# Two pieces of TensorE work taken across stage ends: half of an output product, and a first forward transform

## What is computed

```python
for l in range(DEPTH):                               # DEPTH = 2
    ux = modulate(hx, norm1_g[l], sh1x, sc1x)
    px = ux @ w_in[l]
    ...
    att_x = latent_attention(...)
    hy_x = hyena_branch(px[..., :HY_COLS], sc_w[l], sc_b[l], flt, flt_bias[l])
    hx = hx + g1x * merge_branches(px[..., MLA_END:], hy_x, att_x, w_hy_o[l], w_mla_o[l], w_out[l])
    ...
    hx = hx + g2x * hier_moe(modulate(hx, norm2_g[l], sh2x, sc2x), *moe_w)

def hyena_branch(p_hy, sc_w, sc_b, flt, flt_bias):
    u = short_conv(p_hy, sc_w, sc_b)
    v, x1, x2 = jnp.split(u, 3, axis=-1)
    z = v
    for o, gate in enumerate((x1, x2)):
        z = gate * (long_conv(z, h_freq[:, o]) + flt_bias[o] * z)
    return z

def merge_branches(p_gate, y_hy, y_att, w_hy_o, w_mla_o, w_out):
    g = jax.nn.sigmoid(p_gate)
    return (g[..., :D_MODEL] * (y_hy @ w_hy_o) + g[..., D_MODEL:] * (y_att @ w_mla_o)) @ w_out
```

## Time and profile before

| | us |
|---|---|
| median of three runs | 2640.35 |
| the three runs | 2635.67, 2640.35, 2643.16 |
| the profiled execution | 2635.22 |
| its span | 2633.4 |
| TensorE busy in it | 2422.3 (92%) |
| VectorE busy | 1073.3 (41%) |
| GpSimd busy | 691.3 (26%) |
| ScalarE busy | 621.5 (24%) |
| main transfer queue, share of 16 engines | 55.5% |
| granted TensorE clock, mean | 0.981 of full speed |

### The profile page before, as it was taken

How to read it: one execution, slowest core, us unless ns; L and a number is a source line. 1 busy time by engine, 2 the same in 40 slices (tenths; PEclk the granted TensorE clock), 3 DMA queues, 4 the chain that set the end, 5 groups by cost and what they waited for, 6 DMA issues and landing times. The chain is left out here.

```text
span 2633.4 us, 35470 instructions
## 1 busy us (share of the span) xinstructions
PE 2422.3 (92%) x13020; PEld 1519.3 (58%) x13020; DVE 1073.3 (41%) x2144; ACT 621.5 (24%) x1374; POOL 691.3 (26%) x644
## 2 busy tenths in 40 slices
PE   7999988999999999998888899999999999988887
PEld 3455675555555565555554468645787665555553
DVE  5764487444212663111111175944422732222222
ACT  4441122442110232221111142234211311111111
POOL 0003132565221012222221222246431022222221
PEclk9999999999999999999999999999999999999999
DMA  9982020021113539999999913012226599999996
GB/s 365 372 343 92 28 95 19 14 55 25 48 48 94 233 137 391 395 398 400 402 392 385 360 41 116 33 32 55 49 73 208 233 361 395 392 408 404 403 402 242
DMA packets 192142, 588.40 MB, mean 223 GB/s; under 512 B 48464, under 2 KB 110203, under 8 KB 135708
## 3 DMA queue, kind: packets, MB, share of 16 engines
q1 hardware_dynamic: 167525, 551.99, 55.5%
q0 software_dynamic: 22400, 29.42, 3.4%
q10 hardware_dynamic: 2103, 5.51, 0.5%
HBM read 581.44 MB, written 51.51 MB: 240 GB/s over the span
## 5 line engine op out<-in xcount | busy, mean ns | idle before, releaser
L2661 PE MATMUL ps<-w,moe_xt 128*64 128x256 f32 x2816 | 341.2, 397 | 61.3 <-DMA w<-in_w_up_e 59.0
L2801 POOL DMA_INDIRECT rows_out<-moe_rows_out,table x128 | 117.9, 921 | 738.5 <-DVE moe_rows_out L2866 375.1
L2661 PEld LDWEIGHTS ps<-w,moe_xt 128*64 128x64 f32 x2816 | 221.3, 142 | 150.8 <-issue 67.6
L2916 DVE TENSOR_TENSOR moe_gated<-ps,moe_gated 64x256 f32<-64x256 f32 x128 | 54.5, 426 | 501.0 <-ACT moe_gated L2885 500.9
L2885 ACT ACTIVATE moe_gated<-ps 64x256 f32<-64x256 f32 x128 | 48.2, 376 | 666.9 <-PE ps L2661 666.9
L2661 PE MATMUL ps<-early_w,moe_xt 128*64 128x256 f32 x1280 | 153.4, 394 | 28.3 <-DMA early_w<-in_w_up_e 28.3
L1706 POOL TENSOR_SCALAR attn_p<-attn_p,attn_rs 128x768 f32<-128x768 f32 (+1 forms) x80 | 155.4, 1951 | 81.2 <-DVE attn_rs L1880 80.7
L2669 PE MATMUL ps<-w,moe_ht 128*64 128x512 f32 x704 | 170.4, 604 | 2.3 <-issue 2.3
L2178 PE MATMUL ps<-w_out,mix 128*128 128x512 f32 x320 | 144.6, 602 | 7.0 <-PEq L150 7.0
L2902 DVE TENSOR_TENSOR moe_rows_out<-ps,moe_row_gate 64x512 f32<-64x512 f32 x128 | 88.1, 688 | 138.3 <-PE ps L2669 136.2
L2661 PEld LDWEIGHTS ps<-early_w,moe_xt 128*64 128x64 f32 x1280 | 101.8, 141 | 65.9 <-issue 31.7
(11 more groups left out here) (435 smaller groups left out, 4271.8 us busy)
## 6 DMA issues: line engine op xcount, KB each, us to landing
w<-in_w_gate_e SPq DMA_DIRECT2D x88, 1024.0 KB, 25.9
w<-in_w_up_e SPq DMA_DIRECT2D x88, 1024.0 KB, 29.5
w<-in_w_down_e SPq DMA_DIRECT2D x88, 1024.0 KB, 29.3
prep_w<-in_w_ada SPq DMA_DIRECT2D x24, 2048.0 KB, 16.0
early_w<-in_w_gate_e SPq DMA_DIRECT2D x40, 1024.0 KB, 25.7
early_w<-in_w_up_e SPq DMA_DIRECT2D x40, 1024.0 KB, 29.5
early_w<-in_w_down_e SPq DMA_DIRECT2D x40, 1024.0 KB, 29.7
w_merge<-in_w_in SPq DMA_DIRECT2D x32, 512.0 KB, 5.4
```

The source lines that it names most:

```text
L2661: last = nc.tensor.matmul(ps[k * SLOTS:(k + 1) * SLOTS, 0:DE], xt[:, c], wgu[:, k, c], start=c == 0, stop=c == KC - 1)
L2801: nc.gpsimd.indirect_dma_start(out=dram["y"], out_offset=bass.IndirectOffsetOnAxis(ap=m.table[0:SLOTS, j:j + 1], axis=0), in_=y[:, j % 2], ...
L2916: nc.vector.tensor_tensor(h[:, b % 2], m.ps[SLOTS:2 * SLOTS, b % 2, 0:DE], sg[SLOTS:2 * SLOTS, b % 2], ALU.mult).then_inc(s["h_done"], 1)
```

## The change

Two pieces of TensorE's work are issued in the stage ahead of the one that uses them.

First, the forward transform of job 0 becomes a function `long_forward` and is issued at the end of `hyena_in_stage`, in place of the 16 small matmuls. Before it, TensorE waits for the matrix `dft0`, for the last copies into `m.v`, and for VectorE's last additions out of banks 0 to 3. `forward(0)` in `conv_stage` is left with counting `fwd_done`.

Second, the first half (chunks 0 to 3 of 8) of the first half-product of `out_stage` is issued at the end of `merge_stage`, by a function `out_product` that both stages use. Before it, TensorE waits for the first half of `w_out`, for seven of the eight sums into `m.mix`, and for the last addition out of bank 0. In `out_stage`, tile 0 begins with chunk 4.

```diff
-def hyena_in_stage(nc, m, l, w_in, streams, early, latent, then):
+def hyena_in_stage(nc, m, l, w_in, streams, early, latent, dft0, then):
...
-            keep_warm(nc, m, 4, 16)
+            dft, dft_in = dft0
+            pe.wait_ge(dft_in, 16)
+            pe.wait_ge(s["tr_evac"], 2 * HC)
+            pe.wait_ge(s["u3_done"], NP)
+            pe.wait_ge(s["u2_done"], NP)
+            pe.wait_ge(s["c22_done"], NP)
+            pe.wait_ge(s["c21_done"], NP)
+            long_forward(nc, m, dft, m.v, 0, 0)
...
+def long_forward(nc, m, dft, src, tok0, half):
+
+    cols = slice(half * (HW // 2), (half + 1) * (HW // 2))
+    for e, residue in enumerate(FORWARD):
+        last = nc.tensor.matmul(m.ps[:, e // 2, (e % 2) * (HW // 2):(e % 2 + 1) * (HW // 2)], dft[:, e], src[:, tok0 + residue, cols],
+                                start=True, stop=True)
+    return last
...
             def forward(i):
+                if i == 0:
+                    pe.sem_inc(s["fwd_done"], 1)
+                    return
...
-                    for e, residue in enumerate(FORWARD):
-                        last = nc.tensor.matmul(m.ps[:, e // 2, (e % 2) * HALF:(e % 2 + 1) * HALF], dft[:, e], src[:, tok0 + residue, cols],
-                                                start=True, stop=True)
-                    last.then_inc(s["fwd_done"], 1)
+                    long_forward(nc, m, dft, src, tok0, half).then_inc(s["fwd_done"], 1)
...
+            w_out, w_out_in = out_early
+            pe.wait_ge(w_out_in[0], 16)
+            pe.wait_ge(s["mix_done"], KC - 1)
+            pe.wait_ge(s["c11_done"], KC)
+            out_product(nc, m, w_out, X, 0, 0, range(KC // 2))
...
+def out_product(nc, m, w, bank, tile, half, chunks):
+
+    for c in chunks:
+        last = nc.tensor.matmul(m.ps[:, bank], m.mix[:, tile, c], w[:, half, c], start=c == 0, stop=c == KC - 1)
+    return last
...
-                tile = work[j][1]
-                for c in chunks:
-                    last = nc.tensor.matmul(m.ps[:, 2 * (j % 2) + half], m.mix[:, tile, c], w[:, half, c],
-                                            start=c == 0, stop=c == KC - 1)
+                last = out_product(nc, m, w, 2 * (j % 2) + half, work[j][1], half, chunks)
...
             for j in range(NT):
-                product(j, 0, range(KC // 2))
                 if j >= 1:
+                    product(j, 0, range(KC // 2))
                     turn(j - 1, 0)
```

More of the change, by code:

```diff
@@ L1939, in merge_loads, with merge_stage @@
                       ).then_inc(loaded[b], 16)
-def merge_stage(nc, m, l, a, streams, early, token_sums, then):
+def merge_stage(nc, m, l, a, streams, early, token_sums, out_early, then):
     n_tok = sum(n for _, _, n in streams)
@@ L2551, in conv_loads @@
                     conv_load(sp, conv_early, name, l, 0, consts, dram)
-            hyena_in_stage(nc, m, l, a["w_in"], streams, hyena_early, latent, conv_loads)
+            hyena_in_stage(nc, m, l, a["w_in"], streams, hyena_early, latent, conv_early["dft0"], conv_loads)
             until_conv.close()
@@ L2597, in mixers @@
         out_early = late.enter_context(nc.sbuf_tensor(f"w_out{l}", [P, 2, KC, 4 * P], F32, side="right")), signals("w_out_in", 2)
-        merge_stage(nc, m, l, a, streams, merge_early, token_sums, lambda sp: out_loads(sp, l, a["w_out"], out_early))
+        merge_stage(nc, m, l, a, streams, merge_early, token_sums, out_early, lambda sp: out_loads(sp, l, a["w_out"], out_early))
     return out_early
```

## The result

| | before | changed |
|---|---|---|
| median of five runs of each, us | 2637.18 | 2619.01 |
| all of them, us | 2635.67 to 2643.16 | 2615.79 to 2622.56 |
| profiled execution, us | 2635.22 | 2619.76 |
| its span, us | 2633.4 | 2618.0 |
| granted clock, mean | 0.981 | 0.987 |

The ratio of the times is 0.993, with a 95% interval of 0.9918 to 0.9943: some 18 us faster, where 14.2 were forecast. The median of 2619 lies inside the range, near its lower end. Of the 7 us by which it misses the forecast of 2626, 3.2 are the base (2640.35 was the median of three runs, 2637.18 is that of five) and the rest is gain beyond the four terms.

The account below looks back on a forecast made before the run. Weight transfers and matmuls of the expert stages bound the kernel; what ends earlier ahead moves them forward whole. 3.54 + 2.78 + 5.2 + 2.65 = 14.2 us off 2640.35 gave 2626 us, range 2618 to 2636.

Parts of the forecast that it names:

- convolution, layer 0: Hyena product's end: the transform runs inside VectorE's tail, so ScalarE copies 3.54 us earlier; bounds 2.5 and 3.7.
- output product, layer 0: Merge stage's end: 4 matmuls (3.5 us) fill TensorE's gap, 1.70 us from the clock; together 5.2 us, bounds 0 and 5.3.
- convolution, layer 1: Hyena product's end: the transform closes the stage 0.72 us later, ScalarE's copy comes 2.78 us earlier; bounds 2.0 and 3.5.
- output product, layer 1: Merge stage's end: 3.5 us moved, barrier 0.85 us later, 2.65 us left; bounds 1.8 and 3.5.
- The covers: Stage ends: moved work hidden under VectorE's tail and GpSimd's sum in layer 0, outlasting them by 0.72 and 0.85 in layer 1.
- What was said to be late next: Convolution: transfers there by 340, inverse transform at 344.6. Output product: VectorE waits for gate rows until 862.09, TensorE sets the pace.
- Rival 5: Expert stages: the saturated weight stream runs at a lower rate; 2.1% makes the kernel 8 us slower, about 2649; chance 0.04.
- Rivals 2 and 3: Convolution doesn't follow, 6.3 us lost (0.06); moved work comes too late, barrier moves by what is saved, 2640 (0.05).
- rival 1: Output product's stage: VectorE and the gate rows bound its beginning; 5.2 + 2.65 us lost, 2634; chance 0.10.
- rival 4: Convolution's start: TensorE pauses twice and the clock falls, taking back 5.1 us in both layers, 2631.3; chance 0.04.
- The signs: Changed profile: convolution begins at 325.3 with a product, copy at 325.5; expert stages start 8.7 and 14.2 us earlier.
- The clock's term: Merge stage's end, layer 0: filling the gap removes the clock's fall, 1.70 us; by the skill's rule 0 to 3.4.

Follow-up runs that it names:

- experiment 2: Only the forward transform moved, output product left whole in its stage, against the kernel before: 2629.98 us, 0.9973.
- experiment 3: Only half of the first half-product moved, transform and 16 small matmuls left where they were, against the kernel before: 2625.51 us, 0.9961.
- Experiment 6: Changed kernel with seven instead of four of the first half-product's eight chunks ahead of the barrier: 2624.19 us, 0.9957 of the kernel before.
- Experiment 7: Changed kernel with the transform's wait split, only its last two matmuls waiting for the last addition: 2619.95 us, 0.9935 of the kernel before.
- experiment 4: Kernel before, nothing moved, plus 16 warming matmuls that nobody reads at the merge stage's end: 2634.44 us, 0.9996 of the kernel before.

## Why the prediction was right, step by step

| term | forecast, us | changed kernel, us |
|---|---|---|
| convolution, layer 0 | 3.54 | 9.08 - 5.48 = 3.60 |
| output product, layer 0 | 5.2 | 5.14 |
| convolution, layer 1 | 2.78 | 7.56 - 4.69 = 2.87 |
| output product, layer 1 | 2.65 | 2.56 |
| sum | 14.2 | 14.2 |

The output product's term of layer 0 is the distance from GpSimd's last sum to the end of the first tile's product: 851.67 + 15.67 - 849.51 = 17.83 before, 848.55 + 10.54 - 846.39 = 12.70 now (5.13; 5.14 by VectorE's last product, 844.56 against 847.67). In layer 1 it is 15.58 and 13.02. The two further traces of the changed kernel have the same four values to within 0.01 us, and those of experiments 2 and 3 have their two of them, but for 2.65 instead of 2.56 in layer 1 of experiment 3 (its pause behind the barrier is 0.30 us instead of 0.39).

- **The covers.** The transform lay inside VectorE's tail in layer 0 and closed the stage in layer 1, the eight records lay under GpSimd's sum in layer 0 and outlasted it in layer 1: all four as forecast. The pauses at the two product ends are 0.60 and 0.39 us.
- **What was said to be late next, and wasn't.** The inverse transform waits for VectorE, not for a transfer: 348.18 became 345.19, 3.6 us less by the drift of 0.61 us that the execution had before the place. The gate rows let VectorE start at 858.57, 12.18 us behind GpSimd's sum (12.58 before), and TensorE doesn't wait for it. It isn't free of that rival by much: in the third trace of the changed kernel a later step on the gate rows starts 0.19 us late, and TensorE comes 0.28 us later to the product behind the first logits.
- **Rival 5** is out: 392 and 383 GB/s against 391 and 384. **Rivals 2 and 3** are out by the table. **Rivals 1 and 4** are out for this kernel, the first but for these 0.3 us. Experiment 6 shows where rival 1 begins. Experiment 7 shows the fall of rival 4 and that its price was put too high: the prediction took the longer run of TensorE (2.56 us in each layer) as lost time, and where VectorE sets the pace such a fall cost nothing. In rival 5, 2.1% of 1030 us less the gain are 7.4 us, not 8; nothing hangs on it.
- **The signs.** The product and ScalarE's copy at the convolution's start came at 325.46 and 325.44, less the drift of 0.61 us, where 325.3 and 325.5 were forecast. The last steps of VectorE ahead of the expert stages lie 8.2 us (layer 0) and 17.2 us (layer 1) earlier, with that drift 8.9 and 17.8; forecast were 8.7 and 14.2. The excess in layer 1 is in no term of the sum.
- **What was luck.** The four terms came true one by one. The whole came out 4 us better than their sum and the base 3 us lower than the one taken; both errors have the same sign, and 1 us more of them would have left the range.

**Where the 15.4 between the spans and the 17 between the series come from.** The sum holds for the places; in the traces the rest is falls of the clock elsewhere. I followed every TensorE instruction that both traces have. At the end of the output product's first tile in layer 1 the changed kernel stands 17.8 us ahead of where it stood at 309 us, so 3.6 more than the four terms. Three places make up nearly all of it: the expert stage of layer 0 (0.9), and two at 1655 and 1718 us (0.9 and 1.7), where the kernel before loses more to the clock. The expert stage's start in the timeline of the kernel before, and of the changed one:

```profile
978.77 6.65 PE L2661 MATMUL ps<-w,moe_xt 128*64 128x256 f32 x32 [0.78 <-ACT moe_xt L2872]
```

```profile
970.41 3.67 PE L2687 MATMUL ps<-w,moe_xt 128*64 128x256 f32 x32 [0.78 <-ACT moe_xt L2898]
```

The same 32 records, 3.0 us apart. By 1521 us 2.1 of these 3.0 are given back and 0.9 left: a fall of the clock inside a saturated stage costs little, while the one behind the merge stage of layer 0, where TensorE sets the pace, cost all of its 1.7 us. In the last expert stage another 1.8 us are given back. None of this belongs to the change for certain.

The further traces show whether such a stage swallows what comes early. All twelve have the same 2146 VectorE operations in the same order, so that each can be read against the kernel before, operation by operation. Ahead of layer 0's expert stage (the operation at 950.4 us in the kernel before) the others stand between 10.9 us ahead and 0.5 us behind. Behind the stage (the operation at 1540.4) each has its lead again to within -1.9 and +1.0 us; a straight line through the twelve leads has a slope of 0.95 (standard error 0.07), where 1 is a lead kept whole and 0 one swallowed. From 2069.9 us to VectorE's last operation at 2627.7 the slope is 0.95 as well (0.07), with 0.3 to 4.5 us lost by every kernel against that one execution, the kernel of experiment 4 most. So leads are carried whole, and what is given back doesn't grow with the lead. In the second trace of the changed kernel a fall came into the warming matmuls ahead of the barrier of the expert stage; the first row is of that trace (all 32 records take 6.53 us), the second of the first one. Over the stage its lead went from 10.9 to 9.0 us, where that of the first trace went from 8.2 to 9.2.

```profile
959.89 6.30 PE L178 MATMUL ps<-ident 128*128 128x128 f32 x30
```

```profile
962.32 3.84 PE L178 MATMUL ps<-ident 128*128 128x128 f32 x32
```

Over 143 executions of nine kernels (the kernel before, the changed one and those of experiments 2 to 7) the time follows the mean clock within a kernel by 0.78 us for each 0.001 (standard error 0.10). The kernel before has a mean of 0.9813 over 60 executions and 2636.4 us, the changed one 0.9850 over 17 and 2619.8 us. 3.7 thousandths are 2.9 us, and 16.6 - 2.9 = 13.7 us are left for all that doesn't go with the clock; 0.7 of the 3.7 thousandths are the fall that is itself part of the 14.2. That is a relation, not a cause: why the clock is higher on average is only partly known. The fall that the filled gap removes makes 3.5 us at half the clock, 0.0007 of the mean.

**The clock's term.** The forecast took the clock's gain as 1.70 us, from one fall, and experiment 4 measured 1.70. The Trainium skill ("TensorE: Matmul & The Clock Gate", Part 1) has the switching not tied to the kernel, and the prediction weighed a term of 0 to 3.4 us by that. At this gap no trace shows a change of outcome from one execution to the next: both that leave it open (before and experiment 2) have the fall, and all ten that fill it don't. Two open gaps are few. At other places the traces agree with it. Ahead of the product at 1718.28 TensorE rests for 2.01 to 2.03 us in all twelve traces; in five the clock falls, in seven it doesn't. Of the three traces of the changed kernel one has the fall. The rows are of the kernel before, of the first trace of the changed kernel and of its third, which rests as long as the kernel before and has no fall:

```profile
1718.28 5.37 PE L1791 MATMUL ps<-wv,kvn 128*128 128x512 f32 x8 [2.03 <-PEq L150]
```

```profile
1705.31 3.67 PE L1807 MATMUL ps<-wv,kvn 128*128 128x512 f32 x8 [2.01 <-PEq L150]
```

```profile
1706.90 3.67 PE L1807 MATMUL ps<-wv,kvn 128*128 128x512 f32 x8 [2.03 <-PEq L150]
```

What stays open is the 2 to 4 us by which series differ beyond what the four terms place, here, with the doubled transform and with seven chunks.

## What to carry to other kernels

At a stage end that all engines wait for, measure how long each is idle there; an idle engine can take the next stage's first work, at a gain of that work's whole length as long as the tail covers it, and of the rest of the tail when it doesn't. Take no more than the cover holds: three chunks more held the barrier until 2.33 us behind GpSimd's end, held up every other engine and cost 1.5 us at the two places (4 us by the series). Before paying for a fall of the clock, ask whether TensorE sets the pace there. Measure such a term as a distance between two instructions on either side of the stage end; in three traces of the changed kernel it repeats to 0.01 us, where whole executions of the changed kernel spread over 9 us.

## What the runs showed of the hardware that was not expected

- A pause of some 2 us has two outcomes, and its length doesn't tell which: ahead of one product, after 2.01 to 2.03 us, the clock fell in five traces of twelve, in the same kernel once in three. After 1.82 us it stood, after 2.08 us it fell. After 4.03 us it fell both times; after 2.96 us it stood both times (before and experiment 2).
- A fall makes TensorE's own work 1.7 us longer at three of the places shown (15.67 against 13.97 us, 5.38 against 3.69, 5.37 against 3.67), and 3.0 us at the expert stage's start (6.65 us against 3.67 for 32 records). What of it reaches the end is another matter: all of it behind the merge stage of layer 0, none where VectorE set the pace (experiment 7).
- Seen over whole executions the clock is worth less than at one place. The fall of rows 10 costs 1.70 us and 0.0007 of the mean, so 2.4 us for 0.001; over the 143 executions it is 0.78, a third. A part of the falls lies in the two streaming stages, and of the one fall that was followed there 2.1 of 3.0 us were given back.
